# Compressed keys and values of two hybrid layers: the first matrix in plain fp32, spread over four groups of 32 array columns

## What is computed

```python
NSA_CMP_LEN = 32
NSA_CMP_STRIDE = 16
NSA_CMP_HIDDEN = 4 * HEAD_DIM          # 256

def nsa_compress(t, gidx, pe, w1, w2):
    B = t.shape[0]
    blocks = t[:, gidx] + pe
    flat = blocks.reshape(B, gidx.shape[0], NSA_CMP_LEN * HEAD_DIM)
    return jax.nn.silu(flat @ w1) @ w2

k_cmp = nsa_compress(kc, gidx, cmp_pe[0], cmp_w1[0], cmp_w2[0])
v_cmp = nsa_compress(vc, gidx, cmp_pe[1], cmp_w1[1], cmp_w2[1])
```

## Time and profile before

| what | value |
|---|---|
| time, median of 3 runs | 1832.42 us (1830.93 to 1837.83) |
| span of the profiled execution | 1826.6 us |
| that execution's own time | not recorded apart from its span; the median of the runs is 5.8 us above it |
| PE busy | 1796.0 us, 98% |
| DVE busy | 1242.0 us, 68% |
| ACT busy | 979.4 us, 54% |
| DMA | 302.41 MB, 166 GB/s on the mean |
| mean granted TensorE clock | 0.999 |

### The profile page before, as it was taken

How to read it: one execution, slowest core, us unless ns; L and a number is a source line. 1 busy time by engine, 2 the same in 40 slices (tenths; PEclk the granted TensorE clock), 3 DMA queues, 4 the chain that set the end, 5 groups by cost and what they waited for, 6 DMA issues and landing times.

```text
span 1826.6 us, 35749 instructions
## 1 busy us (share of the span) xinstructions
PE 1796.0 (98%) x15302; PEld 1712.2 (94%) x15302; DVE 1242.0 (68%) x1895; ACT 979.4 (54%) x1493; POOL 68.0 (4%) x32
## 2 busy tenths in 40 slices
PE   7999999999999999999999999999999999999999
PEld 7999998899999999999988999999989889989989
DVE  6775576765767567755767657775766678766676
ACT  6544567355644455445673645445556565556562
POOL 0000011500000000000115000000000000000000
PEclk9999999999999999999999999999999999999999
DMA  8566543233565655565433335665456435446332
GB/s 330 194 196 195 175 150 116 93 128 116 193 191 195 219 190 193 195 196 173 143 112 105 128 119 182 196 196 191 156 162 208 134 109 175 160 147 223 128 114 96
DMA packets 84462, 302.41 MB, mean 166 GB/s; under 512 B 9168, under 2 KB 11728, under 8 KB 84176
## 3 DMA queue, kind: packets, MB, share of 16 engines
q1 hardware_dynamic: 84304, 300.13, 50.0%
HBM read 299.04 MB, written 1.05 MB: 164 GB/s over the span
## 4 chain that ended last, share of the span: by engine, by line
PE 89%; DVE 6%; ACT 4%; issue 1%; DMA 0%; SPq 0%; DVEq 0%; ACTq 0%
PE bank L383 22%; PE bank L390 22%; PE bank L388 22%; PE bank L692 2%; DVE w_lo L1560 2%; PE bank L408 1%; PE bank L407 1%; PE bank L404 1%; PE bank L619 1%; PE bank L1009 1%; PE bank L1060 1%; PE bank L894 1%; PE bank L1030 1%; PE bank L623 1%; PE bank L622 1%
## 5 line engine op out<-in xcount | busy, mean ns | idle before, releaser
L1560 DVE TENSOR_TENSOR w_lo<-ring,w_hi 128x1024 fp32r<-128x1024 f32 x560 | 678.6, 1247 | 93.9 <-ACT w_hi L1126 92.8
L1126 ACT ACTIVATE w_hi<-ring 128x1024 fp32r<-128x1024 f32 x560 | 580.9, 1055 | 245.9 <-PE bank L383 206.2
L383 PE MATMUL bank<-xs,w_hi 128*128 128x256 f32 x2448 | 687.4, 281 | 0.0
L388 PE MATMUL bank<-xs,w_hi 128*128 128x256 f32 (+1 forms) x2454 | 678.4, 277 | 0.0
L390 PE MATMUL bank<-xs,w_lo 128*128 128x256 f32 x2448 | 678.3, 277 | 0.0
L388 PEld LDWEIGHTS bank<-xs,w_hi 128*128 128x128 f32 x2454 | 461.4, 188 | 3.1 <-issue 2.9
L383 PEld LDWEIGHTS bank<-xs,w_hi 128*128 128x128 f32 x2448 | 460.6, 188 | 4.1 <-issue 2.7
L390 PEld LDWEIGHTS bank<-xs,w_lo 128*128 128x128 f32 x2448 | 461.0, 188 | 0.0
L383 PE MATMUL bank<-a,w_hi 128*128 128x256 f32 x704 | 194.3, 276 | 0.0
L388 PE MATMUL bank<-a,w_hi 128*128 128x256 f32 x704 | 194.3, 276 | 0.0
L390 PE MATMUL bank<-a,w_lo 128*128 128x256 f32 x704 | 194.3, 276 | 0.0
(11 more groups left out here) (399 smaller groups left out, 3081.5 us busy)
## 6 DMA issues: line engine op xcount, KB each, us to landing
ring<-in_w SPq DMA_DIRECT2D x560, 512.0 KB, 3.4
arena<-in_mem SPq DMA_DIRECT2D x2, 1024.0 KB, 12.8
const<-in_const SPq DMA_DIRECT2D x1, 1395.0 KB, 15.9
h<-in_x SPq DMA_DIRECT2D x1, 768.0 KB, 7.7
out<-h SPq DMA_DIRECT2D x3, 256.0 KB, 2.5
dec_par<-in_dec SPq DMA_DIRECT2D x1, 615.0 KB, 19.7
h<-in_x SPq DMA_DIRECT2D x1, 256.0 KB, 4.3
out<-h SPq DMA_DIRECT2D x2, 128.0 KB, 2.0
```

What stands on the lines that cost most here:

```text
L383: last = nc.tensor.matmul(o, wh, hi(x, k0 + k), start=k == 0, stop=False, skip_group_check=True)
L388: nc.tensor.matmul(o[:, c:c + piece], wh, lo(x, k0 + k)[:, c:c + piece], start=False, stop=False, skip_group_check=True)
L1126: nc.scalar.activation(w_hi[:, s * UNIT:(s + 1) * UNIT], ring[:, u % RU, :], AF.Copy).then_inc(sems("w_hi"), 1)
L1560: nc.vector.tensor_tensor(w_lo[:, r * UNIT:(r + 1) * UNIT], ring[:, r, :], w_hi[:, s * UNIT:(s + 1) * UNIT].bitcast(F32), ALU.subtract).th ...
```

## The change

It does the first matrix of the compressed network with plain fp32 matmuls straight from the ring, one for each l in place of three. The 32 positions are dealt over four groups of 32 array columns (l mod 4), each with its own 32 rows of `bank[5]`; so four partial sums stand there, and the turn, now a matmul with a matrix `two32` that has four ones in each column, adds them. The silu moves behind the turn. The 16 units concerned (`WHOLE`) are left out by `highs` and `lows`, whose slots and counts now go by the number among the remaining units (`NTH`, `SPLIT`). `flat` gets 32 columns a position (two are zeros), `flat_hi` and `flat_lo` go, and the constant table grows by 32 columns.

```diff
+WHOLE = frozenset(DEC0 + l * DEC_UNITS + U_CMP + n for l in range(LAYERS) for n in range(8))
+SPLIT = [u for u in range(UNITS_ALL) if u not in WHOLE]
+NTH = {u: n for n, u in enumerate(SPLIT)}
...
-        flat, hid, hid_t = take(32, 2 * NCMP), take(2, 2 * NCMP), take(T)
+        flat, hid, hid_g = take(32, 32), take(2, 2 * NCMP), take(T)
...
+            def whole(self, wide):
+                u, pos = divmod(self.n, UB)
+                if pos == 0:
+                    self.w.e.wait_ge(sems(f"landed{u % RU}"), 16 * (u // RU + 1))
+                self.n += wide
+                return ring[:, u % RU, pos * P:(pos + wide) * P], pos == 0
...
-                pe.e.wait_ge(*pe.need('flat_lo', 1))
+                pe.e.wait_ge(*pe.need('flat', 4))
                 for l in range(32):
-                    wh, wl, first = w.two(2)
-                    fh, fl = (f[:, l * 2 * NCMP:(l + 1) * 2 * NCMP] for f in (flat_hi, flat_lo))
-                    o = bank[5][0:2 * NCMP, 0:T]
-                    last = nc.tensor.matmul(o, fh, wh, start=l == 0, stop=False, skip_group_check=True)
+                    g = l % 4 * 32
+                    ws, first = w.whole(2)
+                    last = nc.tensor.matmul(bank[5][g:g + 32, 0:T], flat[:, l, :], ws, start=l < 4, stop=l >= 28,
+                        skip_group_check=True)
                     if first:
                         last.then_inc(sems("unit_begun"), 1)
-                    nc.tensor.matmul(o, fl, wh, start=False, stop=False, skip_group_check=True)
-                    last = nc.tensor.matmul(o, fh, wl, start=False, stop=l == 31, skip_group_check=True)
...
                 for ht in range(2):
-                    last = nc.tensor.transpose(bank[6][:, ht * 2 * NCMP:(ht + 1) * 2 * NCMP],
-                        hid_t[0:2 * NCMP, ht * P:(ht + 1) * P], ident[0:2 * NCMP, 0:2 * NCMP])
+                    last = nc.tensor.matmul(bank[6][:, ht * 2 * NCMP:(ht + 1) * 2 * NCMP],
+                        hid_g[:, ht * P:(ht + 1) * P], C('two32')[:, 0:2 * NCMP], start=ht == 0, stop=True,
+                        skip_group_check=True)
...
-                    if True:
-                        s = u % HU
+                    if u not in WHOLE:
+                        n = NTH[u]
+                        s = n % HU
...
-                        if u >= HU:
-                            self.w.e.wait_ge(sems("unit_begun"), u - HU + 2)
+                        if n >= HU:
+                            self.w.e.wait_ge(sems("unit_begun"), SPLIT[n - HU] + 2)
...
-                a.e.wait_ge(*a.need('flat', 4))
-                nc.scalar.activation(tiles(flat_hi[:, :], 32), flat, AF.Copy).then_inc(*a.tell('flat_hi'))
...
-                for n in range(1, 9):
-                    s.ahead(u0 + U_CMP + n)
+                s.highs(u0 + U_GL + 2)
                 a.e.wait_ge(*a.need('hid_full', 1))
-                nc.scalar.activation(hid_t[0:2 * NCMP, :], bank[5][0:2 * NCMP, 0:T], AF.Silu).then_inc(*a.tell('hid_s'))
+                nc.scalar.activation(hid_g, bank[5][:, 0:T], AF.Copy).then_inc(*a.tell('hid_s'))
+                s.highs(u0 + U_GL + 3)
                 a.e.wait_ge(*a.need('hid_turned', 1))
-                nc.scalar.activation(hid, tiles(bank[6][:, 0:4 * NCMP], 2), AF.Copy).then_inc(*a.tell('hid_e'))
+                nc.scalar.activation(hid, tiles(bank[6][:, 0:4 * NCMP], 2), AF.Silu).then_inc(*a.tell('hid_e'))
...
-                d.e.wait_ge(*d.need('flat_hi', 1))
-                nc.vector.tensor_tensor(tiles(flat_lo[:, :], 32), flat, tiles(flat_hi[:, :], 32).bitcast(F32),
-                    ALU.subtract).then_inc(*d.tell('flat_lo'))
...
-                for n in range(1, 9):
-                    w.ahead(u0 + U_CMP + n)
+                w.lows(u0 + U_GL + 3)
...
-    put("two32", row % 32 == col[:, :8])
+    put("two32", row % 32 == col[:, :32])
```

More of the change, by code:

```diff
@@ L75, in __call__ @@
         return table[:, a:b]
-CONST = Columns(ones=P, eps=1, pad=7, ident=P, bones=P, le=P, ge=P, level=LEVELS * P, rot=P, sbn=P, nge=P, nones=P, causal=T,
-                cmpn=2 * NCMP, cmpm=2 * NCMP, two8=8, two18=18, two32=8, cos=T, sin=T, final=KD)
+CONST = Columns(ones=P, eps=1, pad=15, ident=P, bones=P, le=P, ge=P, level=LEVELS * P, rot=P, sbn=P, nge=P, nones=P, causal=T,
+                cmpn=2 * NCMP, cmpm=2 * NCMP, two8=8, two18=18, two32=32, cos=T, sin=T, final=KD)
 FIRST = P + 8
@@ L93 @@
               pt="v_sb", f_sq="v_sb", q_sq="ab", q_ln="zl", q_rstd="b_e", masks="l_sb", v="y0", fv="a_sb",
-              gf="o_out", gate_e="o_sq", ft="os_out", flat_hi="os_rstd", z_out="ys", hid_s="l_sq",
+              gf="o_out", gate_e="o_sq", ft="os_out", z_out="ys", hid_s="l_sq",
               hid_e="gz_e", kc_sq="l_ln", vc="l_rstd", forget_hi="dte", kcs_ln="eg", kcs_rstd="yy",
@@ L98 @@
               f_ss="sp_sb", raw="sp_sb", qn="g_out", q_sin="y", qr="gcol", flat="dt", xf="mixed", lf="k_out",
-              flat_lo="qkn", z_r="rr", gl_e="kb", fcol="kq", kcn="kend", kc="lt", pc_d="qkd", pcn="xt_up",
+              z_r="rr", gl_e="kb", fcol="kq", kcn="kend", kc="lt", pc_d="qkd", pcn="xt_up",
               nm="x_up", ob="r1", up_out="mix_lo")
 FFN_UNITS = 3 * KF
+WHOLE = frozenset(DEC0 + l * DEC_UNITS + U_CMP + n for l in range(LAYERS) for n in range(8))
+SPLIT = [u for u in range(UNITS_ALL) if u not in WHOLE]
+NTH = {u: n for n, u in enumerate(SPLIT)}
 class Counts:
@@ L325, in build_program @@
         forget_r = rounded("forget", T, arena_at + 4 * at[0])
-        flat_hi = rounded("flat_hi", 64 * NCMP, arena_at + 4 * pairs_at)
         kvc = take(T)
@@ L329, in build_program @@
         zb = take(8, T)
-        flat_lo = rounded("flat_lo", 64 * NCMP, arena_at + 4 * at[0])
-        flat, hid, hid_t = take(32, 2 * NCMP), take(2, 2 * NCMP), take(T)
+        flat, hid, hid_g = take(32, 32), take(2, 2 * NCMP), take(T)
         kc, kcr, kcs, krt, vc = take(NCMP), take(NCMP), take(NCMP), take(NCMP), take(64)
@@ L358, in low_ready @@
             def low_ready(self, u):
-                self.w.e.wait_ge(sems("w_lo"), u + 1)
+                self.w.e.wait_ge(sems("w_lo"), NTH[u] + 1)
+            def whole(self, wide):
[4 more added lines that the diff above has]
+                return ring[:, u % RU, pos * P:(pos + wide) * P], pos == 0
             def two(self, wide=1):
@@ L368, in two @@
                 self.n += wide
-                c, d = (u % HU * UB + pos) * P, (u % RU * UB + pos) * P
+                c, d = (NTH[u] % HU * UB + pos) * P, (u % RU * UB + pos) * P
                 return w_hi[:, c:c + wide * P], w_lo[:, d:d + wide * P], pos == 0
@@ L1556, in lows @@
                 for u in range(self.u, min(upto, UNITS_ALL)):
-                    if True:
-                        s, r = u % HU, u % RU
-                        self.w.e.wait_ge(sems("w_hi"), u + 1)
+                    if u not in WHOLE:
+                        s, r = NTH[u] % HU, u % RU
+                        self.w.e.wait_ge(sems("w_hi"), NTH[u] + 1)
                         nc.vector.tensor_tensor(w_lo[:, r * UNIT:(r + 1) * UNIT], ring[:, r, :],
@@ L2216, in constants @@
     put("eps", np.full((P, 1), EPS))
-    put("pad", np.zeros((P, 7)))
+    put("pad", np.zeros((P, 15)))
     return c
```

## The result

| | before | changed |
|---|---|---|
| time, median | 1831.68 us (1830.81 to 1837.83, 4 runs) | 1855.03 us (1850.82 to 1856.88, 4 runs) |
| ratio | | 1.0113, 95% interval 1.009 to 1.0136 |
| span of the profiled execution | 1826.6 us | 1855.1 us |
| mean granted clock | 0.999 | 0.996 |

The account below looks back on a forecast made before the run. TensorE's issuing, busy 98% of the span, was taken as the bound. Per layer 11.22 - 3.81 - 0.10 - 0.21 = 7.1 us, both 14.2, so 1832.4 - 14.2 = 1818.2 us, range 1813 to 1827.

Parts of the forecast that it names:

- The terms of the stage: Rewritten stretch, per layer: 11.22 us of rounded matmuls removed; 16 rounds of 0.216 us plus edges added, together 3.81 us.
- The wait for the first low part: At the first gate logit, PE waits about 0.1 us a layer for split weights, 0.6 if DVE or ACT slip.
- its 0.21 us: At the turn, four plain records replace the two transposes' records, which took 0.30 us: 0.21 us more per layer.
- the stall before the rotation: PE's wait before L978, behind the stretch: 1.8 us a layer, expected to stay.
- the burst of DMAs: Weight units after the second gate unit, issued together, one per 0.43 us; DMA falls behind for a moment and catches up.
- the sum: Per layer 11.22 - 3.81 - 0.10 - 0.21 = 7.1 us saved; 14.2 us for both layers.
- Rivals 1 and 2: Column groups in the new stretch run two at a time, 1825.0 us, chance 0.13; or one at a time, 1838.8, chance 0.07.
- The dear form of rival 2: Groups one at a time with each weight load exposed, 0.27 us a record: stretch 17.4 us, time 1845 us.
- Added at no cost: a wider constant, 16 KB more on 1395.: The constant table's growth, counted as 16 KB more to load, at no cost in time.
- a wait on w_lo in the ten us behind it: Place to look if the stretch is short but time does not follow; late weights: 1 us a layer, 1820, chance 0.15.
- a granted clock of 0.5: Clock drop in or behind the new stretch: 1.7 to 3.4 us, 1820 to 1822; chance 0.15 of over 1.5 us.
- The range: Whole kernel time of 1813 to 1827 us, taking in most of the two-at-a-time case and leaving out one-at-a-time.

Follow-up runs that it names:

- the kernel with a tile of its own: Changed kernel with the adding matrix in its own tile behind the arena, all other tiles placed as in the kernel before: 1816.81 us, ratio 0.9919.
- the one with a hole of 256 bytes: Kernel before with only 64 unused fp32 columns added behind the constant table: 1831.00 us, ratio 0.9996.
- the blocks: Changed kernel, adding matrix in its own tile, with the 32 positions dealt eight in a row to each column group: 1833.56 us, ratio 1.0009.

## Why the prediction was wrong

**The terms of the stage were right.** Four groups side by side: 16 rounds, L936 at 379 ns a record as L855's, the stretch 4.02 us against 3.81 + 0.10. The wait for the first low part was 0.15 us against 0.1 (in the kernel with a tile of its own 0.43 in the first layer, so it depends on the execution). The turn cost less than its 0.21 us: from the last matmul ahead of it to the first behind it are 0.48 us (1439.42 to 1439.90), where the earlier trace rows have 0.44. Nothing behind the stretch broke: the stall before the rotation is 1.8 us as before, the burst of DMAs made no wait, and from the last z matmul to that rotation it was 26.35 us and is 19.31 (1432.61 to 1451.92): 7.04 us less, where the sum had 7.1. Rivals 1 and 2 are out. (The dear form of rival 2 has a slip: 64 x 0.27 + 0.35 is 17.6 us, not 17.4.) The Trainium skill ("TensorE: Matmul & The Clock Gate", Part 2, step 1) states that matmuls stay in program order; for plain fp32 matmuls in different column groups the runs disagree, since in the blocks three records that stand earlier in the program are overtaken at each change.

**The step that failed** is the line "Added at no cost: a wider constant, 16 KB more on 1395." I priced the constant as bytes to load. Its cost is that it stands ahead of everything that PE streams, and its 128 bytes changed the distance of activations and weights from 192 to 64 modulo 256. That costs 4.4 ns on each rounded matmul of 256 columns, and makes most of the 36 us lost in the encoders. The same 128 bytes with nothing else changed cost 35 us (1866.83 against 1831.70). No rival held it, because I sought every loss in the stretch and behind it. The kernel asserts where `xs` and the arena may lie (64 modulo 128). The change fulfils that, and the prediction passes over it; it may be a sign that somebody had measured places. The trace had a second sign. The same matmuls stepped by 0.113 us in the feed-forward network and by 0.118 in pieces of the decoder, and the prediction itself uses two steps, 0.113 for the gate units and 0.116 for the old stretch, without asking what sets them.

**What I said would show me wrong** was half of it: "if it is short and the time does not follow: then look for a wait on w_lo in the ten us behind it, or a granted clock of 0.5." The time did not follow, and neither of the two was it. The clock adds a little to the difference of the two profiled spans: the mean granted clock is 0.996 against 0.999, three short drops to 0.5 more (3.4 us each, 1.7 us lost), some 5 us of the 28. One is in the encoder, two follow the stalls at the rotation. They can't be laid to the slower step: the executions of the kernel before have anything from 0.995 to 0.999, and the one with a hole of 256 bytes has 0.996 with the short step in three of its four networks.

**The range** was made of what the stage could do. It held the good version (1816.8) and could not hold 1855.

## What to carry to other kernels

A new constant or buffer is an edit of every address behind it: put it behind all the tiles that the matmuls stream, or pad it to the period (256 bytes here), and count the records of an untouched stretch in both profiles first, since one number (here 113 or 118 ns a matmul) tells this loss at once. Plain fp32 matmuls with up to 32 stationary columns are worth spreading over column groups where each writes its own rows, but deal them in turns, one matmul to a group. When a change is slower and its own stage is faster, undo side effects one at a time before giving it up.

## What the runs showed of the hardware

- Rounded 256-column matmuls in a stream start 113.3, 117.8, 118.7 or 120.0 ns apart, for distances 192, mostly 64, 128 (120.0 in one network of four) and 0 modulo 256 bytes between the streaming tile and its weights; moving both together by 128 bytes changed nothing. In the first network the two first steps come at either distance. The step is the same while DVE and ACT are idle, and while no DMA runs (117.8 and 117.7 ns). That TensorE's two reads of SBUF, of the streaming tile and of the weights, disturb each other is my reading of this; no run shows it by itself. The Trainium skill says in "TensorE: Matmul & The Clock Gate" (Part 2, step 1) that the two read ports are independent and "Loading the next tile's weights doesn't steal SBUF read bandwidth from the running matmul"; if the reading is right, the runs speak against it, by up to 6%.
- Four column groups of plain fp32 run without loss beside each other: 64 records in 16 rounds of 0.216 us, though they read four fp32 tiles at once, twice what L1060 does. The Trainium skill's 2.38 for three column tiles (same page, Part 3) would, by an estimate from that figure, have made the stretch 0.9 us longer (3.46/0.79); the stretch of 4.02 us shows no such loss.
- With 16 records in a row to each column group, a new group's first record starts beside the old one's fourth from last, no earlier (52 rounds for 64 records, at all three changes).
